# Encoder block with 32 routed experts: attention places moved by one, tokens routed in two pairs, roots on ScalarE

## The reference

```python
def reference(x, ...):
    xn = rmsnorm(h, norm_mix_g[l])
    zu, zv, q, k, va, ga, gb = jnp.split(xn @ w_in[l], split_idx, axis=-1)
    y_a = gmlp_spatial_gating(gelu(zu), gelu(zv), ...) @ w_branch_a[l]
    att = sliding_window_attention(q, k, va, attn_sinks[l])   # 8 chunks of 64 tokens, 16 heads
    y_b = att @ w_branch_b[l]
    h = h + (g_a * y_a + g_b * y_b) @ w_out[l]
    hn = rmsnorm(h, norm_ffn_g[l])
    h = h + hierarchical_moe(hn, ...)
    return rmsnorm(h, norm_final_g)

def hierarchical_moe(x, ...):
    glog = xf @ w_rg + b_rg                      # 4 groups, the best one is used
    elog = (elog_all of the chosen group)        # 8 experts in it, top 2
    topv, topi = lax.top_k(elog, TOP_K)
    tw = jax.nn.softmax(topv, axis=-1) * pg
    for e in range(N_EXPERTS):
        h = jax.nn.silu(xf @ w_gate[e]) * (xf @ w_up[e])
        y = y + combine[:, e:e + 1] * (h @ w_down[e])
```

## Time and profile before

| | before |
|---|---|
| median of 3 runs | 897.48 us |
| the profiled execution | 897.09 us |
| its span, first to last instruction | 895.4 us |
| mean granted clock of PE | 0.979 |
| busy, share of the span | PE 94%, PEld 61%, DVE 48%, ACT 26%, POOL 1% |
| HBM read | 245.04 MB |

### The profile page before, as it was taken

The page is one execution under the profiler, slowest core; times in us unless marked ns, Lnnn a source line. Parts: engine busy times, 40 slices in busy tenths (PEclk is TensorE's granted clock), DMA queues, the critical chain, the costliest instruction groups (busy, mean ns, idle before and its releaser), DMA issues.

```text
span 895.4 us, 11442 instructions
## 1 busy us (share of the span) xinstructions
PE 844.7 (94%) x4635; PEld 550.3 (61%) x4635; DVE 427.2 (48%) x824; ACT 230.3 (26%) x423; POOL 7.6 (1%) x24
## 2 busy tenths in 40 slices
PE   8999999999999999999999969999994799999975
PEld 7888888877777888888834324544531353644632
DVE  5538325677765344436769244135133224335133
ACT  6322222464443222213304111110110100100114
POOL 0000000000000100000000000000000000000000
PEclk9999999999999999999999979999996899999998
DMA  8544312212122743695999999999999999999994
GB/s 298 143 94 111 104 51 94 94 48 95 48 95 49 229 130 94 238 399 232 370 374 372 401 427 430 427 427 427 426 429 429 426 428 427 429 426 427 427 410 184
DMA packets 72407, 250.01 MB, mean 279 GB/s; under 512 B 23032, under 2 KB 46624, under 8 KB 59168
## 3 DMA queue, kind: packets, MB, share of 16 engines
q1 hardware_dynamic: 71984, 248.18, 71.3%
q0 software_dynamic: 288, 1.05, 0.3%
q10 hardware_dynamic: 80, 0.02, 0.0%
HBM read 245.04 MB, written 4.20 MB: 278 GB/s over the span
## 4 chain that ended last, share of the span: by engine, by line
PE 87%; DMA 9%; DVE 2%; ACT 1%; issue 1%; SPq 0%; DVEq 0%; ACTq 0%
PE bank L1045 18%; PE bank L720 10%; PE bank L722 10%; PE bank L721 10%; PE bank L1104 8%; DMA R<-w_down 5%; DMA R<-w_up 3%; PE bank L749 2%; PE bank L748 2%; PE bank L747 2%; PE bank L1132 2%; PE bank L1009 2%; PE by_side L1009 2%; PE bank L1133 2%; PE bank L1091 2%; PE bank L851 1%
## 5 line engine op out<-in xcount | busy, mean ns | idle before, releaser
L1045 PE MATMUL bank<-R,packT 128*64 128x512 f32 (+1 forms) x972 | 184.7, 605 | 14.4 <-DMA R<-w_up 13.3
L1045 PEld LDWEIGHTS bank<-R,packT 128*64 128x64 f32 (+1 forms) x972 | 58.0, 128 | 123.3 <-issue 122.8
L1667 DVE TENSOR_TENSOR wlo<-raw,whi 128x2048 fp32r<-128x2048 f32 x33 | 75.5, 2288 | 84.8 <-ACT whi L1325 84.7
L720 PE MATMUL bank<-xnT_hi,whi 128*128 128x512 f32 x288 | 113.2, 393 | 0.0
L722 PE MATMUL bank<-xnT_hi,wlo 128*128 128x512 f32 x288 | 112.1, 389 | 0.0
L721 PE MATMUL bank<-xnT_lo,whi 128*128 128x512 f32 x288 | 112.1, 389 | 0.0
L1104 PE MATMUL bank<-R,actT 128*64 128x512 f32 (+1 forms) x384 | 76.4, 658 | 13.7 <-DMA R<-w_down 13.5
L1325 ACT ACTIVATE whi<-raw 128x2048 fp32r<-128x2048 f32 x33 | 63.1, 1912 | 68.4 <-PE by_side L722 33.8
L1104 PEld LDWEIGHTS bank<-R,actT 128*64 128x64 f32 (+1 forms) x384 | 23.0, 137 | 62.0 <-issue 61.3
L720 PEld LDWEIGHTS bank<-xnT_hi,whi 128*128 128x128 f32 x288 | 54.1, 188 | 11.3 <-issue 0.6
L722 PEld LDWEIGHTS bank<-xnT_hi,wlo 128*128 128x128 f32 x288 | 54.1, 188 | 11.3
(11 more groups left out here) (416 smaller groups left out, 1324.9 us busy)
## 6 DMA issues: line engine op xcount, KB each, us to landing
R<-w_up SPq DMA_DIRECT2D x27, 2048.0 KB, 20.8
R<-w_gate SPq DMA_DIRECT2D x25, 2048.0 KB, 20.8
R<-w_down SPq DMA_DIRECT2D x21, 2048.0 KB, 21.5
raw<-w_in SPq DMA_DIRECT2D x17, 1024.0 KB, 5.1
R<-w_down SPq DMA_DIRECT2D x12, 1024.0 KB, 14.3
R<-w_gate SPq DMA_DIRECT2D x14, 512.0 KB, 7.6
raw<-w_in SPq DMA_DIRECT2D x20, 256.0 KB, 4.6
R<-w_up SPq DMA_DIRECT2D x5, 1024.0 KB, 9.2
```

Source lines behind the costliest of these rows:

```text
L720: pe.matmul(dst, hi_w, hi_x, start=start, stop=False)
L1045: mm = pe.matmul(dst[s * w:(s + 1) * w, :], packT[:, side, c, s * w:(s + 1) * w], part_of(s, c) if part_of else slots[s // 2].tiles[s % 2] ...
L1667: dve.tensor_tensor(wlo[c % 2][:, :], raw[c % 2][:, :], whi[c % 2][:, :].bitcast(F32), ALU.subtract).then_inc(lo_split, 1)
```

## The change

Four things. (1) The attention slots begin at g = 4, so each slot comes one tile earlier: 0 to 3 with g = 4 to 7, then 4 + 4u + m and 6 + 4u + m. (2) The gain of the norm is no longer multiplied in by DVE on all of h (`gain_h`, its 512 KB constant `ffn_g` and its load are gone); h is scaled by 1/rms alone, and the gain is applied when rows are copied to `packT`: four copies of 128 columns with a scale on ACT, one multiplication on DVE. (3) The roots of h are taken by ACT, with one Newton step on DVE; ACT makes all the copies of turned h; DVE scales tile 0, ACT tiles 1 to 3. (4) The tiles are routed in two pairs: ranks, masks and the gather of tiles 0, 1 come ahead of those of 2, 3. PE's products that only kept it busy (`keep_warm`) go, some fills remain. SP stores tile 0 ahead of the last loads that wait for the last unit, tile 1 behind them, and tiles 2, 3 behind `R[6]`; `gate_fifth` waits for the first mask of tile 2.

```diff
     gate_rest = at("gate_rest", [P, 2 * DE], F32, 200)
     first_down = [at(f"first_down{half}", [P, 4 * DE], F32, kb) for half, kb in enumerate((24, 136))]
-    hn_first = at("hn_first", [P, 2, TT, KT // 2, P], F32, 128)
...
+            sp.wait_ge(first_hn_ready, 1)
+            store_rows(0, first_stored)
             sp.wait_ge(dve_tile_done, 24)
             sp.dma_start(R[7][:, 4 * DE:8 * DE], flat(w_gate, 3)[:, 4 * DE:8 * DE]).then_inc(slot_loaded[3], 16)
             sp.dma_start(ninth[:, 4 * DE:8 * DE], flat(w_up, 3)[:, 4 * DE:8 * DE]).then_inc(up_ahead, 16)
             sp.dma_start(tenth[:, 4 * DE:8 * DE], flat(w_down, 1)[:, 4 * DE:8 * DE]).then_inc(slot_loaded[2], 16)
-            for t in range(TT):
-                sp.wait_ge(hn_ready, t + 1)
-                sp.dma_start(hn_rows[1 + t * P:1 + (t + 1) * P, :].rearrange("q (a n) -> q a n", a=2),
-                             hn_first[:, :, t, :, :].rearrange("q a c p -> q a (c p)")).then_inc(hn_stored, 16)
+            sp.wait_ge(hn_ready, 1)
+            store_rows(1, first_stored)
             sp.wait_ge(hsq_summed, 2 * TT)
             sp.dma_start(gate_tail[:, :], flat(w_gate, 0)[:, 6 * DE:8 * DE]).then_inc(slot_loaded[0], 16)
             sp.wait_ge(logits_done, TT)
             sp.dma_start(gate_sixth[:, :], flat(w_gate, 0)[:, 5 * DE:6 * DE]).then_inc(slot_loaded[0], 16)
             sp.dma_start(R[6][:, :], flat(w_gate, 2)).then_inc(slot_loaded[3], 16)
-            sp.wait_ge(masks_ready, 1)
+            for t in range(2, TT):
+                sp.wait_ge(hn_ready, t)
+                store_rows(t, hn_stored)
+            sp.wait_ge(masks_ready, 3)
             sp.dma_start(gate_fifth[:, :], flat(w_gate, 0)[:, 4 * DE:5 * DE]).then_inc(fifth_loaded, 16)
-            sp.wait_ge(hn_stored, 16 * (TT + 1))
+            sp.wait_ge(hn_stored, 16 * 3)
             sp.wait_ge(right_turned, 1)
             sp.dma_start(first_down[1][:, :], flat(w_down, 0)[:, 4 * DE:8 * DE]).then_inc(spare_loaded, 16)
...
-                    if g >= 5:
-                        attention_slot(g - 5)
+                    if g >= 4:
+                        attention_slot(g - 4)
...
+                    attention_slot(4 + 4 * u + m)
                 for m in range(2):
                     if u == 0 and m == 0:
                         pe.wait_ge(sp_ready, KT)
                     d = 2 * u + m
                     pe.wait_ge(gate_used, 8 + d)
                     tall_tile(GA + 2 * u + 1, m, bank[2][:, :], spT_hi, spT_lo, dve_tile_done)
-                    attention_slot(5 + 4 * u + m)
+                    attention_slot(6 + 4 * u + m)
 
             for u in range(4):
                 for m in range(2):
...
-                    pe.wait_ge(hgT_a, t - 1)
-                    pe.wait_ge(hgT_b, t - 1)
+                    pe.wait_ge(hgT_copied, 2 * t - 2)
                 for c in range(KT):
-                    mm = pe.transpose(bank[4 + 2 * (t % 2) + c // 4][:, (c % 4) * P:(c % 4 + 1) * P],
...
-                    pe.wait_ge(hgT_b, t + 1)
-                else:
-                    pe.wait_ge(hgT_c, 1)
+                pe.wait_ge(hgT_copied, 2 * t + 2)
+                if t >= 2:
+                    pe.wait_ge(logits_ready, t - 1)
                 for c in range(KT):
-                    mm = pe.matmul(bank[t][:, 0:NR], hgT[t // 2][:, c, (t % 2) * P:(t % 2 + 1) * P],
+                    mm = pe.matmul(logits_psum(t), hgT[t // 2][:, c, (t % 2) * P:(t % 2 + 1) * P],
                                    w_router[:, c, :], start=(c == 0), stop=(c == KT - 1))
                 mm.then_inc(logits_done, 1)
...
+                    pe.matmul(dst, all_ones[:, :], spaced_row[:, :], start=True, stop=False)
+                    for tp in range(t + 1):
+                        mm = pe.matmul(dst, earlier[:, :] if tp == t else all_ones[:, :],
+                                       picked[:, tp, :], start=False, stop=(tp == t))
+                mm.then_inc(ranks_done, 1)
+
             def turn_first_tiles():
-                for t in range(2):
-                    turn_h(t)
+                turn_h(0)
+                turn_h(1)
 
             for c in range(WO, UNITS):
...
                     for c in range(4):
-                        mm = pe.matmul(bank[2 + n][:, c * P:(c + 1) * P], hn_first[:, n, t, c, :], onehot_first[:, t, :],
+                        mm = pe.matmul(bank[2 + n][:, c * P:(c + 1) * P], hn_first[:, t, 4 * n + c, :], onehot_first[:, t, :],
                                        start=(t == c == 0), stop=(t == TT - 1), skip_group_check=True)
-                mm.then_inc((left_turned, right_turned)[n], 1)
+                if pair:
+                    mm.then_inc((left_turned, right_turned)[n], 1)
 
             def gather_rows(line, g):
...
+            rank_tiles(1)
+            for t in range(TT):
+                mm = pe.matmul(bank[6][:, 0:NE], all_ones[:, :], picked[:, t, :], start=(t == 0), stop=(t == TT - 1))
+            mm.then_inc(ranks_done, 1)
+            for _ in range(2):
                 fill(256, 4)
-            pe.wait_ge(hn_ready, TT)
-            gather_first(0)
+            pe.wait_ge(hn_ready, TT - 1)
+            gather_first(1, 0)
             number_rows(1, 1)
-            gather_first(1)
+            gather_first(1, 1)
             def run_round(i):
 
                 odd = i % 2
...
                     if g in (5, 7):
                         start_unit(GA - 1 if g == 5 else GA)
-                    if g >= 5:
-                        attention_slot(g - 5)
+                    if g >= 4:
+                        attention_slot(g - 4)
...
-            def copy_hgT(t, half):
+            def copy_hgT(t):
                 act.wait_ge(hgT_psum, t + 1)
-                act.activation(hgT[t // 2][:, 4 * half:4 * half + 4, (t % 2) * P:(t % 2 + 1) * P],
-                               bank[4 + 2 * (t % 2) + half][:, :].rearrange("p (c q) -> p c q", c=4),
-                               ACT.Copy).then_inc(hgT_c if half else hgT_a, 1)
-
+                for half in range(2):
+                    act.activation(hgT[t // 2][:, 4 * half:4 * half + 4, (t % 2) * P:(t % 2 + 1) * P],
+                                   bank[HGT_BANKS[t][half]][:, :].rearrange("p (c q) -> p c q", c=4),
+                                   ACT.Copy).then_inc(hgT_copied, 1)
+
+            def scale_h(t):
+                act.wait_ge(rstd_ready, t // 2 + 1)
+                act.activation(hn_first[:, t, :, :], h_tok[:, t, :].rearrange("q (p c) -> q c p", c=KT),
+                               ACT.Copy, scale=rstd[:, t:t + 1]).then_inc(hn_ready, 1)
+
...
-            copy_hgT(0, 0)
-            copy_hgT(1, 0)
+            root_h(0)
+            copy_hgT(0)
+            copy_hgT(1)
             square_h(1, 2)
-            scale_h(0)
             scale_h(1)
             square_h(1, 3)
-            copy_hgT(2, 0)
-            copy_hgT(3, 0)
-            copy_hgT(3, 1)
+            copy_hgT(2)
+            root_h(1)
+            copy_hgT(3)
             scale_h(2)
             scale_h(3)
             act.wait_ge(route_sub, 1)
...
-                    act.activation(packT[:, 0, 4 * n:4 * n + 4, :], bank[b][:, :].rearrange("p (c q) -> p c q", c=4),
-                                   ACT.Copy).then_inc((main.pack_a, main.pack_b)[n], 1)
-                    return
+                    act.wait_ge(late_loaded, 16 * 5)
+                    act.wait_ge(first_stored, 16 * 2)
                 for c in range(4):
-                    last = act.activation(packT[:, 1, 4 * n + c, :], bank[b][:, c * P:(c + 1) * P], ACT.Copy,
+                    last = act.activation(packT[:, r // 3, 4 * n + c, :], bank[b][:, c * P:(c + 1) * P], ACT.Copy,
                                           scale=gain_pc[:, 4 * n + c:4 * n + c + 1])
                 last.then_inc((main.pack_a, main.pack_b)[n], 1)
 
...
 
                 part = slice(2 * pair, 2 * pair + 2)
                 dve.wait_ge(hsq_summed, TT + 2 * pair + 2)
...
+                dve.scalar_tensor_tensor(out=mean_sq[:, part], in0=half_sq[:, part], scalar=EPS,
+                                         in1=half_sq[:, TT + 2 * pair:TT + 2 * pair + 2], op0=ALU.add,
+                                         op1=ALU.add).then_inc(h_mean_ready, 1)
+                dve.wait_ge(h_mean_ready, pair + 1)
+
+            def rstd_h(pair):
+
+                part = slice(2 * pair, 2 * pair + 2)
+                y, value, work = rstd[:, part], mean_sq[:, part], root_work[:, part]
+                dve.wait_ge(root_ready, 4 + pair)
+                then(dve.reciprocal(y, x_root[:, part]))
+                then(dve.tensor_tensor(work, y, value, ALU.mult))
+                then(dve.scalar_tensor_tensor(out=work, in0=work, scalar=-0.5, in1=y, op0=ALU.mult, op1=ALU.mult))
+                dve.scalar_tensor_tensor(out=y, in0=work, scalar=1.5, in1=y, op0=ALU.add, op1=ALU.mult).then_inc(rstd_ready, 1)
+                dve.wait_ge(rstd_ready, pair + 1)
 
             def low_h(t):
```

(30 more changed lines are left out.)

244 lines of the change are left out of this document (114 added, 130 removed).

## The result

| | before | changed |
|---|---|---|
| median of 6 runs each | 896.98 us (896.03 to 898.97) | 901.28 us (900.22 to 901.85) |
| ratio to before, 95% interval | | 1.0045 (1.0033 to 1.0056) |
| profiled execution, its span | 897.09, 895.4 us | 901.02, 899.3 us |
| mean granted clock of PE | 0.979 | 0.974 |

What follows compares the result with a forecast made beforehand. The weights' stream was taken to bound from about 506 us, PE's program to move the end before that. Attention +1.1 and routing with copies -0.6 gave +0.5 us, forecast as 898.0 us against the median 897.48; range 895.0 to 900.3.

Steps and rivals of the forecast that it cites:

- 0.1 for the restart: Attention, PE behind the new wait at slot 4: restarting costs 0.1 us on top of 3.1 us of waiting.
- 32 products took 3.81 us and are 32 again: Routing, PE's gather of pair 0: the same 32 products take 3.81 us again, from 434.7 to 438.4.
- Bound and transfer to the end: Weights' stream bounds from about 506 us; PE's time at about 473 us moves the end one to one.
- Part 1: Attention one place earlier: -2.6 waits removed, +0.5 at u = 3, +3.2 at slot 4; sum +1.1 us, bounds +0.5 to +1.7.
- Part 2: Roots and gains: worth nothing by itself; DVE can start choosing for pair 0 at about 429.9 us.
- Part 3: Routing in two pairs: DVE's next masks start at 440.9 us as before; PE's c = 4 comes 1.1 us earlier.
- Part 4: Four copies with the gain: +0.15 us ahead of `project_down` in round 0, +0.43 us in round 2.
- Part 5: SP's queue: tile 0's store is hidden; `gate_fifth`, issued at 440.7 us, may take 9.2 and lands in time.
- (a): Rival, SP's loads: `gate_fifth` lands late, at 451.5, and delays c = 4; 899.6 us, chance 0.20.
- (b): Rival, attention: no wait at slot 4, since ACT and DVE catch up in g = 4 to 7; 894.8 us, chance 0.13.
- (c): Rival, routing: its gain is hidden by the stream or twice as large; 898.6 or 897.4 us, 0.63 together with the forecast.
- (d): Rival, ACT: a table switch directly behind exponentials costs 1.4 us more, once in the chain; 899.4 us, chance 0.04.

Runs made afterwards that it cites:

- e4: Changed kernel plus twelve unused 128-column products on PE in the wait ahead of the scores of slot 4; median 898.13 us, ratio 1.0009 to before.
- e3: Changed kernel plus one unused 512-column product on PE ahead of the ranks of pair 0; median 898.78 us, ratio 1.0010 to before.
- e5: Changed kernel plus unused PE products in both places, twelve at slot 4 and one ahead of the ranks of pair 0; 896.62 us, ratio 0.9989 to before.
- e9: Changed kernel run again with no edit, in a later group of runs; median 900.77 us, ratio 1.0027 to before.
- e1: Kernel before with only the attention slots moved one place earlier on PE, ACT and DVE; median 899.54 us, ratio 1.0025 to before.
- e6: Kernel before with its idle products, `keep_warm(3)`, deleted; ratio 1.0003 to before.
- e7: Kernel before with slot 7 right behind slot 6, so slots come one place earlier only from u = 1; median 896.59 us, ratio 0.9989 to before.

## Why the prediction was wrong

**The step that failed: durations of PE's work, taken at full clock, in two terms.** The sum has "0.1 for the restart" behind the new wait and "32 products took 3.81 us and are 32 again" in the routing. The clock fell to half in both places, and the falls cost 1.6 us (e4) and 3.1 us (e3) on top.

**Bound and transfer to the end: right.** Stretches I to III sum to +4.5 us in the changed kernel, the profiled execution is 3.9 us longer than that of the kernel before, and the ratio says 4.0. PE's delay ahead of 500 us reached the end nearly one to one.

**Part 1: mechanism right, two terms mis-sized, one missing.** The wait of 3.1 us came (3.08), released by DVE's read of step 3, and the Gelus of g = 5 to 7 stood at 164.67, 173.72 and 183.04 (forecast 164.9, 173.95, 183.3). Without the clock's fall the part is +0.2 us and not +1.1 (e4, e5): each removed wait gave back 1.07 us, as the two branch tiles of a unit took 12.16 us before and take 5.53 and 5.56 now, where I had counted 0.87; and u = 3 cost 0.2 instead of 0.5. A wait is shown only from the end of a product, 0.39 us after its issue, where issues are 0.23 us apart: 0.16 of the 0.2 I missed. The +0.2 lies outside my bounds of +0.5 to +1.7. The missing term is the clock: 1.6 us behind the wait in the first profile, 3.0 in e9. That the part came to +1.8, near +1.1, is in part luck: 0.9 too much against 1.6 missing. I had put down "0.1 for the restart", the price of a wait of 0.8 us, for one four times as long.

**Part 2: right.** In e5, where stretch I ends when it did before, DVE starts choosing for pair 0 at 429.80 (forecast 429.9), and stretch II shows no cost of the roots and the gains.

**Part 3: right but for the clock.** With the clock held (e5), `picked` was done at 432.43 and 437.80 (forecast 432.5 and 437.9), the masks at 440.83 (440.9), c = 4 at 449.82 (449.95), and DVE waited 0.77 us for the ranks (0.5). In the changed kernel the clock turns -1.2 into +1.9 us. The 3.81 us of the 32 products is a duration read at full clock, in a kernel whose idle products the change removes. The removal of `keep_warm` has no line in my sum at all.

**Part 4: right, a little small.** +0.15 and +0.43 were forecast; the waits ahead of `project_down` of round 0 (0.89 instead of 0.73 us) and of round 2 (0.89 instead of 0.34) make 0.7, stretch III 0.7 to 0.8:

```profile
502.81 1.49 PE L1051 MATMUL bank<-R,packT 128*32 128x512 f32 x12 [0.89 <-ACT packT L1540]
```

**Part 5: right.** `gate_fifth` landed 5.8 us after its issue in the changed kernel; in e5 it was issued at 440.68 (forecast 440.7) and took 7.7 us, less than the 9.2 allowed. DVE ends the wait at c = 4 in both.

**The rivals.** (a) falls with that, (b) with the wait at slot 4, (c) with the -1.2 us of stretch II at full clock (e3, e5), neither hidden nor doubled. (d), a dearer switch of tables, falls too; this is the one added ahead of g = 5, on ACT:

```profile
163.38 1.28 ACT L1352 ACT_TABLE_LOAD   x1
164.67 0.60 ACT L1352 ACTIVATE gbuf<-bank 128x512 f32<-128x512 f32 x1
```

From the load to the next activation 1.29 us, as before, though exponentials stand right ahead of it. The 2.66 us of the Trainium skill (ScalarE: Activation LUTs, What ACT_TABLE_LOAD costs) don't show here either. None of the rivals had the clock of PE in it: with each of them the time stays below 900.3. The corrected sum is +0.2 + 1.6 - 1.2 + 3.1 + 0.7 = +4.4 us, of which 4.7 are the clock's.

## What to carry to other kernels

Durations of PE read from a trace hold for the clock that stands beside them: where a change adds a wait of microseconds, or takes idle products out and puts narrow ones in their place, give the sum a second line at half clock, and count it where another engine waits for that work. A fall costs little where PE waits anyway (0.2 us of the 1.7 missing from full clock in e1's routing, 0.7 of 3.4 in e6) and nearly all that is missing where its products set the time or gate another engine (1.6 of 1.7 at slot 4, 3.1 of 3.4 in the changed routing). Products without use, in waits that are there anyway, took both falls away at no cost that the stretches show; better still is an order without the wait (e7).

## What the runs showed of the hardware that I had not expected

The granted clock fell to the lower level behind a wait as short as 0.86 us when products of 36 and 32 columns stood around it (changed kernel), and in e1 behind such products with no wait at all; in both profiles of the kernel before it did not fall behind the same products, nor behind the 1.17 us of idle time ahead of its ranks. One program had falls of different length in different executions: behind slot 4 the windows show 1.7 us in all missing from 1.00 in the first profile and 3.4 in e9. The Trainium skill (TensorE: Matmul & The Clock Gate, Part 1: The HAM clock gate) says of a kernel's start that how many products run at the low clock varies from run to run. These runs show the same in a kernel's middle, with the falls of different length and with 895.8 to 902.7 us for the changed kernel in e9, against 896.2 to 898.3 for the kernel before beside it. Such a kernel wants more runs than six: its ratio was 1.0045 in one series and 1.0027 in another. What decides in a given execution whether the clock falls stays open.
